# The modulation product as matrix multiplies on TensorE, and the first stage as a pipeline over eight slices of the model width

## The reference, cut to what matters

```
silu_c = silu(c); silu_cc = silu(c_ctx)
for l in range(2):
    sh, sc, gt    = split(silu_c  @ w_ada[l] + b_ada[l], 3)      # w_ada[l]: 1024 x 3072, fp32
    shc, scc, gtc = split(silu_cc @ w_ada[l] + b_ada[l], 3)
    h  = rms_norm(x,   norm_pre[l]) * (1 + sc)  + sh
    hc = rms_norm(ctx, norm_pre[l]) * (1 + scc) + shc
    y, yc = attn_mixer(h, hc, ...) if l == 0 else ssm_mixer(...)
    x = x + gt * rms_norm(y, norm_post[l]);  ctx = ctx + gtc * rms_norm(yc, norm_post[l])
```

## Time and profile before

| | |
|---|---|
| median of 3 runs | 1746.29 us (1729.85 to 1750.39) |
| span of the profiled execution | 1742.8 us, 3.5 below the median |
| first stage and keys/values, to the first scores | 0 to 220.0 us |
| attention | 220 to 782 us |
| out projection of layer 0, layer 1 | 782 to 1742.8 us |
| busy shares of the span | PE 85%, PEld 75%, DVE 56%, ACT 44%, POOL 38% |

### The profile page before, as it was taken

How to read it: one execution, slowest core, us unless ns; L and a number is a source line. 1 busy time by engine, 2 the same in 40 slices (tenths; PEclk the granted TensorE clock), 3 DMA queues, 4 the chain that set the end, 5 groups by cost and what they waited for, 6 DMA issues and landing times.

```text
span 1742.8 us, 23696 instructions
## 1 busy us (share of the span) xinstructions
PE 1476.3 (85%) x8564; PEld 1305.3 (75%) x8564; DVE 978.6 (56%) x1620; ACT 761.3 (44%) x1552; POOL 657.7 (38%) x448
## 2 busy tenths in 40 slices
PE   0477789989998999969995899898898989897797
PEld 0466678888888888858874787888887887887576
DVE  7764464665556555644206566666657676666232
ACT  4433234444444444532316454454545555544331
POOL 5443243333333433322233253535435353534133
PEclk9988888999998999989997999998989999996699
DMA  7332211211211121114411111111101111110341
GB/s 255 123 119 97 73 37 51 86 46 45 69 67 45 45 79 58 46 62 159 160 43 63 48 49 45 52 36 48 60 24 60 36 60 36 48 61 12 139 146 66
DMA packets 37813, 124.39 MB, mean 71 GB/s; under 512 B 5248, under 2 KB 5504, under 8 KB 37760
## 3 DMA queue, kind: packets, MB, share of 16 engines
q1 hardware_dynamic: 33152, 113.20, 19.0%
q10 hardware_dynamic: 4608, 10.49, 1.9%
HBM read 108.99 MB, written 14.68 MB: 71 GB/s over the span
## 4 chain that ended last, share of the span: by engine, by line
PE 46%; DVE 18%; issue 14%; POOL 11%; ACT 9%; DMA 2%; ACTq 0%; DVEq 0%; POOLq 0%; SPq 0%
PE psL L1748 10%; POOL wlo L1529 4%; PE psC L1748 4%; PE psS L1723 3%; PE psS L1725 3%; PE psS L1724 3%; DVE Yst L1056 3%; PE psV L1723 3%; POOL xw L1701 3%; PE psL L2004 2%; PE psV L1725 2%; PE psV L1724 2%; PE psT L2088 2%; PE psL L1723 2%; PE psT L1849 2%
## 5 line engine op out<-in xcount | busy, mean ns | idle before, releaser
L1529 POOL TENSOR_TENSOR wlo<-wraw,whi 128x1024 fp32r<-128x1024 f32 x120 | 295.6, 2464 | 566.4 <-ACT whi L579 317.1
L1748 PE MATMUL psL<-hhi,whi 128*128 128x512 f32 x320 | 133.3, 416 | 0.0
L1748 PE MATMUL psL<-hlo,whi 128*128 128x512 f32 x320 | 131.4, 411 | 0.0
L1748 PE MATMUL psL<-hhi,wlo 128*128 128x512 f32 x320 | 131.1, 410 | 0.0
L1748 PE MATMUL psC<-hhi,whi 128*128 128x256 f32 x320 | 99.0, 309 | 28.6 <-ACT QR L626 21.0
L2004 PE MATMUL psL<-h1hi,whi 128*128 128x512 f32 x256 | 105.6, 412 | 0.0
L2004 PE MATMUL psL<-h1lo,whi 128*128 128x512 f32 x256 | 102.9, 402 | 0.0
L1193 DVE TENSOR_TENSOR PTlo<-psT,PThi 128x256 fp32r<-128x256 f32 (+3 forms) x96 | 68.2, 710 | 61.9 <-ACT PThi L708 61.2
L1723 PE MATMUL psV<-PThi,Vhi 128*128 128x256 f32 (+1 forms) x224 | 72.5, 324 | 35.5 <-DVE PTlo L1193 24.5
L2004 PE MATMUL psL<-h1hi,wlo 128*128 128x512 f32 x256 | 102.6, 401 | 0.0
L708 ACT ACTIVATE PThi<-psT 128x256 fp32r<-128x256 f32 (+3 forms) x96 | 58.8, 612 | 97.2 <-PE psT L1849 95.9
(11 more groups left out here) (369 smaller groups left out, 4911.5 us busy)
## 6 DMA issues: line engine op xcount, KB each, us to landing
wraw<-in_w_ssm SPq DMA_DIRECT2D x48, 512.0 KB, 3.3
wraw<-in_w_in SPq DMA_DIRECT2D x40, 512.0 KB, 3.9
wraw<-in_w_out SPq DMA_DIRECT2D x32, 512.0 KB, 4.0
wraw<-in_w_ada_late SPq DMA_DIRECT2D x27, 512.0 KB, 3.3
wraw<-in_w_ada SPq DMA_DIRECT2D x16, 512.0 KB, 4.3
X<-in_xc SPq DMA_DIRECT2D x12, 512.0 KB, 8.5
y_spill<-Yst SPq DMA_DIRECT2D x16, 384.0 KB, 2.5
X<-y_spill ACTq DMA_DIRECT2D x16, 384.0 KB, 3.2
```

Of the source, the lines that this page charges most:

```text
L1529: G_.tensor_tensor(wlo[:, par], wraw[:, slot], f(whi[:, par]), ALU.subtract).then_inc(s_weight_lo, 1)
L1748: last = PE_.matmul(out, a, b, start=i == 0, stop=i == 3 * KT - 1, skip_group_check=True)
```

## The change

The modulation moves to PE. A tile now lies with its 1024 input rows in the partitions (eight blocks of 128x128) and is the stationary side of eight matmuls; the moving side is silu(c), 128x2 (both vectors at once). Tile and vector stay fp32. The sums for a tile collect in two columns of the psV bank, and DVE applies bias and the factor 0.5 from there.

The first stage runs slice by slice. All 16 early tiles have a place of their own (`ada`), in pairs (shift and scale of slice k), so their loads wait for nothing. On PE, for each k: the 16 matmuls of the pair, the six transposes, and the projection of slice k-1 for both kinds of e = 0 and both token groups. Squares and scaling of X0 are shared between ACT and DVE. The 32 late tiles are all taken in attention, one in each of the first two `values` of a head, right ahead of its own matmuls. For e = 1..3, kind 1's context part moves to psS, so it no longer waits for the copy of kind 0's.

The diff, cut to its core:

```diff
@@ sync engine @@
-        for v in range(2):
-            sp.dma_start(csilu[:, v], io["cvec"][v].partition_broadcast(P)).then_inc(s_small_loaded, 16)
+        sp.dma_start(csilu[:], io["cvec"]).then_inc(s_small_loaded, 16)
...
+        for k in range(KT):
+            for n in (2 * k, 2 * k + 1):
+                sp.dma_start(ada[:, n], io["w_ada"][n]).then_inc(s_ada_pair_loaded[k], 16)
+            if k == 0:
+                w_in_load(0)
+                w_in_load(1)
         sp.wait_ge(s_h_lo, KT)
         sp.dma_start(costab[:], io["cos"]).then_inc(s_tables_loaded, 16)
...
+        late_loads(0)
+        for u in range(2, 2 * GROUPS + 2):
+            sp.wait_ge(s_weight_lo, u - 1)
+            w_in_load(u)
@@ vector engine @@
-                V_.tensor_tensor_reduce(out=product, in0=place, in1=csilu[:, v, :], scale=0.5, scalar=0.0,
-                                        op0=ALU.mult, op1=ALU.add, accum_out=mod[:, tile, v:v + 1]).then_inc(s_modulation_tile_done, 1)
...
+        def modulation_columns(k):
+            dve.wait_ge(s_modulation_tile_done, 2 * k + 2)
+            V_.scalar_tensor_tensor(mod[:, k:ADA_EARLY:KT, :], mod_bank(0, ADA_EARLY)[:, k:ADA_EARLY:KT, :], 0.5,
+                                    bcast2(col("b_ada", 0, ADA_EARLY)[:, k:ADA_EARLY:KT], 2), ALU.mult,
+                                    ALU.add).then_inc(s_modulation_columns, 1)
+            dve.wait_ge(s_modulation_columns, k + 1)
+            V_.scalar_tensor_tensor(gain[:, 0, k, :], mod[:, KT + k, :], 1.0, col("pre", k).broadcast_to([P, 2]),
+                                    ALU.add, ALU.mult).then_inc(s_gain_columns, 1)
+        modulation_columns(0)
+        dve.wait_ge(s_rstd, 1)
+        for t in range(1, TT, 2):
+            V_.tensor_scalar(X0[:, t, :], X0[:, t, :], rstd[:, 0, t:t + 1], None, ALU.mult).then_inc(s_x_normed, 1)
+        modulation_columns(1)
         for k in range(KT):
 ...
+            if k + 2 < KT:
+                modulation_columns(k + 2)
@@ POOL and ACT, in attention (POOL's multiply, ACT's sum) @@
-                    G_.tensor_tensor(product0[:], wraw[:, 2 + hs % 2].rearrange("p a b -> p (a b)"), csilu[:, v, :],
-                                     ALU.mult).then_inc(s_modulation_product, 1)
-                    A_.activation(product0[:], product0[:], ACT.Copy, scale=0.5,
-                                  accum_out=modp[:, hs, v:v + 1]).then_inc(s_modulation_product_summed, 1)
@@ tensor engine @@
         def ctx_bank_free(e, kind):
-            if kind == 0:
-                if isinstance(e, int) and e <= GROUPS:
-                    if e:
-                        pe.wait_ge(s_tanh_ctx, e)
-                else:
-                    pe.wait_ge(s_gate_ctx, e - GROUPS)
+            early = isinstance(e, int) and e <= GROUPS
+            if kind == 0 and early:
+                pe.wait_ge(s_q_ctx_evacuated, e)
+                pe.wait_ge(s_tanh_ctx, 1)
+            elif kind == 0:
+                pe.wait_ge(s_gate_ctx, e - GROUPS)
+            elif early and e < GROUPS:
+                pe.wait_ge(s_tanh_ctx, e)
             else:
                 pe.wait_ge(s_q_ctx_evacuated, e + 1)
...
+        def modulate(tile, place):
+            for k in range(KT):
+                last = PE_.matmul(psV[:, MODS + 2 * place:MODS + 2 * place + 2], tile[:, k, :], csilu[:, k, :], start=k == 0,
+                                  stop=k == KT - 1, skip_group_check=True)
+            last.then_inc(s_modulation_tile_done, 1)
+        for k in range(KT + 1):
+            if k < KT:
+                pe.wait_ge(s_ada_pair_loaded[k], 32)
+                if k:
+                    pe.wait_ge(s_modulation_columns, k)
+                modulate(ada[:, 2 * k], k)
+                modulate(ada[:, 2 * k + 1], KT + k)
+                if k == 0:
+                    pe.wait_ge(s_x_normed, TT)
+...
+            if k:
+                if k == 1:
+                    tile_ready(0)
+                    tile_ready(1)
+                pe.wait_ge(s_h_lo, k)
+                for kind in (1, 0) if k > 1 else (0, 1):
+                    project(0, kind, 0, 3 * k - 3, 3 * k, kind, (s_q_ctx_proj, s_g_ctx_proj)[kind])
+                for kind in range(2):
+                    project(0, kind, 1, 3 * k - 3, 3 * k, kind, (s_q_lat_proj, s_g_lat_proj)[kind])
...
@@ values(r, pair), after its waits and ahead of its matmuls @@
+            if pair == 0:
+                pe.wait_ge(s_late_modulation_columns, r + 1)
+            if q < 2:
+                pe.wait_ge(s_raw_weights_loaded[2 + q], 16 * (GROUPS * r + hs + 1))
+                modulate(wraw[:, 2 + q], 2 * hs + q)
```

More of the change, by code:

```diff
@@ L90, in build @@
     mod = sbuf(keep, "mod", [P, 2 * ADA, 2])
-    modp = sbuf(keep, "modp", [P, GROUPS, 2])
+    csilu = sbuf(keep, "csilu", [P, KT, 2])
+    cth = sbuf(keep, "cth", [P, KT, 2])
     gain = sbuf(keep, "gain", [P, 2, KT, 2])
@@ L281, in build @@
     W_OUT0 = NW_KV + 2 * HEADS
[L282 to L292, removed]
+    LATE = 2 * ADA - ADA_EARLY
+    assert LATE == 2 * HEADS
+    USES_HEAD0 = NW_KV // 2
+    USES_OUT0 = [USES_HEAD0 + HEADS] * 2 + [HEADS] * 2
     STORED = 32
@@ L305, in build, with mod_bank, ctx_bank @@
     SLOTS = GROUPS * BLOCKS
[L308 to L329, removed]
+    MODS = 2 * P
+    def mod_bank(first, n):
+        return psV[:, MODS + 2 * first:MODS + 2 * (first + n)].rearrange("p (a v) -> p a v", v=2)
+    def ctx_bank(e, kind):
+        if kind and isinstance(e, int) and 0 < e < GROUPS:
+            return psS[:, 0:CTX]
+        return psC[:, kind * CTX:(kind + 1) * CTX]
     def col(name, i=0, n=1):
@@ L1727, in _ @@
         pe.wait_ge(s_constants_made, 4)
-        pe.wait_ge(s_x_normed, TT)
-        for k in range(KT):
-            ps = (psS, psT)[k % 2]
-            if k >= 2:
-                pe.wait_ge(s_h_scaled, k - 1)
-            for t in range(TT):
-                last = PE_.transpose(ps[:, t * P:(t + 1) * P], X0[:, t, k * P:(k + 1) * P], ident[:])
-            last.then_inc(s_x_transposed, 1)
         def project(e, kind, part, k0, k1, w, done):
@@ L1740, in project @@
             toks = slice(0, CTX) if part == 0 else slice(CTX, TOK)
-            out = psC[:, 0:CTX] if part == 0 else psL[kind][:, :]
+            out = ctx_bank(e, kind) if part == 0 else psL[kind][:, :]
+            shared = isinstance(e, int) and e == 0 and part == 0 and kind == 1
             for i in range(k0, k1):
                 k, m = divmod(i, 3)
-                if m == 0 and kind == 0 and part == 0 and isinstance(e, int) and e == 0:
-                    pe.wait_ge(s_h_lo, k + 1)
                 a = (whi, whi, wlo)[m][:, par, k, :]
                 b = (hhi, hlo, hhi)[m][:, k, toks]
-                last = PE_.matmul(out, a, b, start=i == 0, stop=i == 3 * KT - 1, skip_group_check=True)
+                last = PE_.matmul(out, a, b, start=i == 0 and not shared, stop=i == 3 * KT - 1, skip_group_check=True)
                 if i == 3 * KT - 1:
```

220 lines of the change are left out of this document (58 added, 162 removed).

## The result

The changed kernel takes 1825.5 us (median of 4 runs, 1818.3 to 1836.2), against 1748.3 (1729.9 to 1750.4) for the kernel before in the same session: a ratio of 1.048, 95% interval 1.040 to 1.055. It is slower. The forecast was 1796 us, range 1725 to 1835, with 0.60 on slower by over 2%. One run of a later kernel (128 columns in the late matmuls) took 1961.2 us at a granted clock of 0.73, where its four others took 1782.3 to 1798.9 at 0.91 to 0.92; it is left out of what follows.

A forecast was written before the change was run, and what follows sets the result against it. Three stages had three limits: DVE's dot products first, then PE with gaps, then PE nearly the limit in attention. Terms of -13 before attention and +66 in it gave +53 on 1746.3, so 1799, shaded to 1796 us; range 1725 to 1835.

The forecast's parts named there:

- Price of a product: Modulation on PE: an fp32 product is two instructions of 0.105 us; a tile 1.68 us at full clock, 3.4 at half.
- rival 4: Modulation tiles on PE: weight loads hide behind one another, 0.4 us a tile; kernel 1705 to 1735 us; chance 0.03.
- Clock in the first stage: First stage: modulation tiles don't keep the full clock, so slices go back and forth; e = 0 ends at 98 us.
- rival 1: Modulation on PE: two-column matmuls hold the clock; first stage ends at 72 us, kernel 1742 us; chance 0.20.
- First stage, +4: Slices up to e = 1: last hlo at 95, then 13.3 us for load and conversion; e = 1 starts at 108, not 104.43.
- Keys and values, -16.5: e = 1 to 4: bank change and unstretched dgk save 19 us; e = 1 starting at half clock costs 2.5.
- Attention, +66: Attention stage: added PE work 54 us, lost clock 27, relief -15; between +14 and +92.
- 32 groups of 16 matmuls: Attention: 32 late tiles on PE at 1.68 us each add 54 us.
- clock: (130 - 79)/2: Attention: 8 further clock falls of 6.8 us, each losing half, add 27 us (ends 0 and 38).
- relief of POOL and ScalarE: Attention: removing their products un-stretches DVE operations, 20 us, three quarters reaching PE: -15 us (ends 0 and -40).
- (2): Attention isn't PE's limit but the scores-to-PTlo chain's; PE's waits vanish; kernel 1665 to 1705 us; chance 0.12.
- (3): Attention and slices: every burst costs the clock and slices run at half; kernel 1841 us; chance 0.12.

The follow-up runs named there:

- The lighter kernel before: Kernel before, with POOL's 32 attention modulation products and ScalarE's 32 sums of them cut from 1024 to 16 columns: ratio 1.000.
- the four repairs: Changed kernel with 128 columns in early and late modulation matmuls, e = 1 weights loaded ahead of tables, hhi/hlo ahead of next slice's columns: 1756.0 us, ratio 1.008.
- SP's order mended: Against the kernel with repaired first stage and late tiles off PE: two late tiles loaded early, weight loads ahead of late tiles' loads: 1707.5 us, ratio 0.977.

## Why the prediction was right, and which terms were off

**Verdict and cause: right.** It is slower by more than 2%, by matmuls added to an engine that was nearly the limit, and by the clock that they cost. The forecast's sum was +53, the spans say +74 and the medians +77, so 1825.5 us lies within the stated range but above the forecast's own 1775 to 1820.

**Price of a product: right.** 0.105 and 0.21 us from start to start; 32 take 6.97 us at half clock. 128 columns cost nearly the same (32 in 3.58 us, 0.112 each). The Trainium skill ("TensorE: Matmul & The Clock Gate", Back-to-back issue gap) gives about 25 ns for 1 to 64 columns, in a formula for an isolated gap that by its own words has no budget for the weight load; these matmuls have one each, and the rows go the other way, so rival 4 falls.

**Clock in the first stage: right in kind.** The slices go back and forth, 9.6 to 12.8 us each. The pairs with 128 columns keep the full clock from 31.06 us on, so it is the two columns that don't, and rival 1 falls.

**First stage, +4: measured +12.5; the overlap was wrong in one place.** e = 1 starts at 116.94 instead of 104.43. From the end of the last `hlo` (103.1) it is 13.8 us, where I had 13.3 (the terms named there add up to 12.9). But the last `hlo` was to be done at 95. I had put "ACT 1.2, DVE 1.5 us" beside PE's work and had not read DVE's order, in which `hhi` and `hlo` stand behind the columns of the next slice, and so behind its tiles. With the order turned round the last `hlo` is done at 91.9. The first transposes also came 2.3 us later than the 24 of the forecast: the pair was there 1.0 us later, and DVE's first small operation on `gain` (L974) took 2.03 us, where later ones take 0.16. (DVE's dot products that fall away are 22 and not 21; nothing hangs on it.)

**Keys and values, -16.5: measured -18.4** (115.6 to 97.1 us from e = 1 to the first scores), and the bank alone is worth 15.7.

**Attention, +66: measured +80.** Worked out from the runs' terms:

| Term | forecast | from the runs |
|---|---|---|
| 32 groups of 16 matmuls, 1.70 to 1.81 us each at full clock | +54 | +56 |
| clock: (130 - 79)/2 | +27 | +25.5 |
| relief of POOL and ScalarE, as PE's idle time: 54.2 to 51.2 | -15 | -3 |
| wider spacing of 128x512: 720 at 0.2332 instead of 0.2307 us | none | +2 |
| sum | +66 | +80.5 |

The mis-sized term is the relief. I had put DVE's stretched operations at 20 us and let three quarters of it reach PE. The lighter kernel before shows 9.5 us less of DVE's work, and next to nothing of it in PE's idle time. The reason is argued and not shown: a stretched operation lay beside PE's work, and the waits of the earlier trace rows come of the chain from scores to PTlo itself. The same four terms give for 128 columns 56 - (79 - 49)/2 - 1 + 2 = +42 (measured +43), and for the groups behind V, 1.70 us each there, 54 + (99 - 79)/2 - 1 + 2 = +65 (measured +67). That the clock's term came out as forecast is in part luck: I had 8 more falls of 6.8 us; it was 7 more, and 51 us more at half clock.

**Rivals.** (1) falls by the half clock measured. (2) falls by the relief: without POOL's products PE's waits stay at 24.5 + 12.2 us. (3) comes nearer in time, 1841, than the forecast, but not by its mechanism: not every group costs the clock (13 of 32 have a fall behind them), and the slices went back and forth. (4) falls by the price.

**Open:** why the kernel with the bank's wait has 34 us more at half clock; why 128x512 matmuls in keys and values stand 0.233 us apart in the changed kernel and 0.228 in the kernel before.

## What to carry to other kernels

Moving work to TensorE pays in a stage where it waits and costs in one where it is the limit; a change that does both should be split. Here, with all tiles on TensorE and the four repairs the ratio was 1.008, with the late tiles back on the other engines 0.987, and with SP's order mended 0.977. A matmul of 2 columns cost as much time here as one of 128 (0.105 and 0.112 us) and kept the full clock less well, so if it must be on TensorE, try it with the columns that are nearly free. Before giving a gain to a relieved engine, ask whether the limiting engine's waits end on it; and in a pipeline, read each engine's program order, since an operation queued behind something not yet due can set the period.

## What the runs showed that I had not expected

- Matmuls of 128 columns instead of 2 made a stage 37 us shorter with the same count of them, and the clock accounts for it (0.96 instead of 0.90 over it).
- The place of the same few-column matmuls matters by itself: between other matmuls instead of behind a wait of PE's, half clock is 31 us less.
- Taking 70 us of POOL's and 27 us of ScalarE's work out of attention left the time as it was, ratio 1.000.
- The time at half clock in attention depends on what lies ahead of it, by no rule that I can give: 165 us with the bank's wait put back and a start 16 us later, 147 with a start 19 us earlier, 130 with starts 6 and 10 us earlier, as in the changed kernel.
